# A two-model transformer block on one Trainium2 core: vector-engine order in the third and last mixers

## The reference

```python
# third mixer, per head (4 heads of 512 channels), written by chunks of 64 tokens in the reference
num = einsum(q k^T * w_intra, v) + w_inter * (C q)
den = s.sum(-1) + w_inter * (n . q)
h = num / max(|den|, exp(-m_row))
hn = (h - mean(h)) * rsqrt(var(h) + eps)
y = (hn * ln_w + skip * x_conv) * silu(z)
x = x + y @ w_out

# last mixer, 16 heads of 64 channels
q, k_c, v_c, k_s, v_s, k_w, v_w, z, g_logit = split(h @ w_in)
o = gate0 * o_cmp + gate1 * o_sel + gate2 * o_win      # three softmax attentions
x = x + (o * silu(z)) @ w_out
```

## Time and profile before

| | |
|---|---|
| median of 3 runs | 944.97 us (944.79 to 946.65) |
| the profiled execution | 943.69 us, its span 942.0 us |
| PE busy | 929.2 us, 99% of the span |
| DVE, ACT, POOL busy | 661.7, 531.6, 79.0 us |
| granted TensorE clock | 0.998 |
| chain that ended last | PE 85%, DVE 9%, ACT 3% |

### The profile page before, as it was taken

How to read it: one execution, slowest core, us unless ns; L and a number is a source line. 1 busy time by engine, 2 the same in 40 slices (tenths; PEclk the granted TensorE clock), 3 DMA queues, 4 the chain that set the end, 5 groups by cost and what they waited for, 6 DMA issues and landing times.

```text
span 942.0 us, 16082 instructions
## 1 busy us (share of the span) xinstructions
PE 929.2 (99%) x5908; PEld 813.3 (86%) x5908; DVE 661.7 (70%) x1107; ACT 531.6 (56%) x946; POOL 79.0 (8%) x104
## 2 busy tenths in 40 slices
PE   9999999999999999999999999999999999999997
PEld 9999888888888987888888888999888789999885
DVE  4978667555464897665545466997778876689985
ACT  6654465444444677654445446666545754377783
POOL 0000011111110000100000000000010006522200
PEclk9999999999999999999999999999999999999999
DMA  8655557656555323766555543533222575322312
GB/s 319 219 189 180 201 185 234 213 178 228 200 197 194 115 88 112 258 214 208 213 180 190 193 166 122 179 136 134 69 90 90 198 271 185 128 80 100 111 46 90
DMA packets 43692, 157.78 MB, mean 168 GB/s; under 512 B 5468, under 2 KB 6252, under 8 KB 42864
## 3 DMA queue, kind: packets, MB, share of 16 engines
q1 hardware_dynamic: 41664, 147.99, 45.3%
q0 software_dynamic: 1824, 8.45, 2.6%
q10 hardware_dynamic: 144, 0.52, 0.2%
HBM read 155.50 MB, written 1.05 MB: 166 GB/s over the span
## 4 chain that ended last, share of the span: by engine, by line
PE 85%; DVE 9%; ACT 3%; issue 1%; DMA 0%; POOL 0%; ACTq 0%; SPq 0%; DVEq 0%
PE ps L758 9%; PE ps L762 9%; PE ps L760 8%; PE ps L537 8%; PE ps L590 7%; PE ps L538 7%; PE ps L539 7%; PE ps L594 7%; PE ps L592 7%; DVE wl L1741 2%; PE ps L575 1%; PE ps L773 1%; PE ps L577 1%; PE ps L579 1%; PE ps L1124 1%
## 5 line engine op out<-in xcount | busy, mean ns | idle before, releaser
L1741 DVE TENSOR_TENSOR wl<-raw,wh 128x1024 fp32r<-128x1024 f32 x270 | 330.5, 1241 | 108.1 <-ACT wh L1210 59.9
L1210 ACT ACTIVATE wh<-raw 128x1024 fp32r<-128x1024 f32 x174 | 181.9, 1057 | 105.5 <-DMA raw<-stream_dram 90.6
L537 PE MATMUL ps<-hxa,wh 128*128 128x256 f32 x672 | 196.5, 292 | 1.1 <-DVE nq L1791 0.8
L538 PE MATMUL ps<-hxa,wh 128*128 128x256 f32 x672 | 189.9, 283 | 0.0
L539 PE MATMUL ps<-hxa,wl 128*128 128x256 f32 x672 | 189.8, 282 | 0.0
L758 PE MATMUL ps<-wh,hxa 128*128 128x512 f32 x352 | 139.1, 395 | 0.0
L762 PE MATMUL ps<-wl,hxa 128*128 128x512 f32 x352 | 137.3, 390 | 0.0
L537 PEld LDWEIGHTS ps<-hxa,wh 128*128 128x128 f32 x672 | 128.4, 191 | 10.1 <-issue 5.4
L760 PE MATMUL ps<-wh,hxa 128*128 128x512 f32 x352 | 137.0, 389 | 0.0
L1378 ACT ACTIVATE wh<-raw 128x1024 fp32r<-128x1024 f32 x96 | 100.0, 1058 | 50.9 <-DMA raw<-stream_dram 33.3
L538 PEld LDWEIGHTS ps<-hxa,wh 128*128 128x128 f32 x672 | 128.6, 191 | 0.1
(11 more groups left out here) (364 smaller groups left out, 1288.5 us busy)
## 6 DMA issues: line engine op xcount, KB each, us to landing
raw<-stream_dram SPq DMA_DIRECT2D x271, 512.0 KB, 4.0
biasm<-bias_dram POOLq DMA_DIRECT2D x12, 192.0 KB, 3.7
w<-w_dram POOLq DMA_DIRECT2D x1, 2048.0 KB, 10.6
mlw<-mlw_dram POOLq DMA_DIRECT2D x1, 1056.0 KB, 6.5
x<-x_dram SPq DMA_DIRECT2D x1, 1024.0 KB, 7.0
mem<-memT_dram SPq DMA_DIRECT2D x1, 1024.0 KB, 8.2
memx<-mem_dram SPq DMA_DIRECT2D x1, 1024.0 KB, 6.0
grow<-rows_dram POOLq DMA_DIRECT2D x2, 512.0 KB, 3.8
```

The costliest lines, as they stand in the source:

```text
L537: pe.matmul(o, wh[:, w_s, w_cols], act[hi], start=start, stop=False, skip_group_check=True)
L538: pe.matmul(o, wh[:, w_s, w_cols], act[lo], start=False, stop=False, skip_group_check=True)
L1210: act.activation(wh[:, v % RING, :], raw[:, v % RAW, :], ACT.Copy).then_inc(wh_ready, 1)
L1741: dve.tensor_tensor(wl[:, s % RING, :], raw[:, s % RAW, :], wh[:, s % RING, :].bitcast(F32), ALU.subtract).then_inc(wl_ready, 1)
```

## The change

It moves instructions on DVE and ACT and adds none; PE's and SP's programs are the same.

- Third mixer, DVE: for h = 2 the two operations of the denominator stand directly behind the decays of head 3, ahead of `low` and `take` of chunk z 9, the low parts of y and `weigh(3)`. In the last head `gated(4, 7)` and `gated(7, 9)` become `gated(4, 8)` and `gated(8, 9)`: the step c = 7 stands ahead of the reciprocal of line 2280.
- Last mixer, DVE: what stood at the end of pair p (an `ahead`, and the low part of y(p-2) for p of 2 and more) becomes `n_behind(p)`, called for p = 1 to 4 in the pair behind, between its two `n_maxima`. For p = 5 it stays at the end.
- Last mixer, ACT: in pair 0 `n_window(0)` and `n_window(1)` stand ahead of the `split` of line 1210.

```diff
@@ ACT
+                if p == 0:
+                    n_window(0)
+                    n_window(1)
                 for e in N_FILL[p][1:2]:
                     ahead_of(PN[e], e)
-                if p < N_PAIRS - 1:
+                if 0 < p < N_PAIRS - 1:
                     n_window(2 * p)
-                n_window(2 * p + 1)
+                if p:
+                    n_window(2 * p + 1)
@@ DVE, third mixer (denominator(h) is the block removed below)
                 if h + 1 < ML_HEADS:
                     decays(h + 1)
+                if h == 2:
+                    denominator(h)
                 if 1 <= h < ML_HEADS - 1:
                     gate_chunks(*Z_BEFORE[h])
@@
                 if h + 1 < ML_HEADS:
                     weigh(h + 1)
 
-                dve.wait_ge(ml_rows_copied, h + 1)
-                dve.wait_ge(ml_summed, h + 1)
-                link(dve.tensor_tensor(h_a[:], ps[:, 4, 0:T], h_em[:, h % 2, :], ALU.max))
-                e = dve.scalar_tensor_tensor(out=h_a[:], in0=ps[:, 4, 0:T], scalar=-1.0, in1=h_a[:],
-                                             op0=ALU.mult, op1=ALU.max)
-                e.then_inc(ml_den_ready, 1)
+                if h != 2:
+                    denominator(h)
                 dve.wait_ge(ml_den_ready, h + 1)
                 link(dve.reciprocal(h_r[:], h_a[:]))
@@
                 if h == ML_HEADS - 1:
-                    gated(4, 7)
+                    gated(4, 8)
                 dve.wait_ge(ml_std_ready, h + 1)
                 link(dve.reciprocal(h_a[:], h_t[:]))
                 if h == ML_HEADS - 1:
-                    gated(7, 9)
+                    gated(8, 9)
@@ DVE, last mixer
+            def n_behind(p):
+
+                ahead(PN["q", p + 2].u if p < 3 else PN["z", p].u)
+                if p >= 2:
+                    low_part(n_y[:], p - 2, Y_N + p - 2)
+
@@
                 n_maxima(2 * p)
+                if 2 <= p <= 5:
+                    n_behind(p - 1)
                 n_maxima(2 * p + 1)
@@
                     n_probs(2 * p + 1)
-                    ahead(PN["q", p + 2].u)
                 else:
@@
                     n_probs(2 * p + 1)
-                    ahead(PN["z", p].u)
-                if p >= 2:
-                    low_part(n_y[:], p - 2, Y_N + p - 2)
+                if p == 5:
+                    n_behind(p)
```

More of the change, by code:

```diff
@@ L2233, in add_skip, with denominator @@
                 dve.tensor_tensor(xc, xc, h_sq[:], ALU.add).then_inc(ml_done, 1)
+            def denominator(h):
+                dve.wait_ge(ml_rows_copied, h + 1)
+                dve.wait_ge(ml_summed, h + 1)
+                link(dve.tensor_tensor(h_a[:], ps[:, 4, 0:T], h_em[:, h % 2, :], ALU.max))
+                e = dve.scalar_tensor_tensor(out=h_a[:], in0=ps[:, 4, 0:T], scalar=-1.0, in1=h_a[:],
+                                             op0=ALU.mult, op1=ALU.max)
+                e.then_inc(ml_den_ready, 1)
             take(PM["z", 2], z_of(2), Rm)
```

## The result

| | before | changed |
|---|---|---|
| median | 944.82 us (8 runs) | 947.47 us (8 runs, 947.28 to 948.13) |
| ratio to before | | 1.0026, 95% interval 1.0017 to 1.0034 |
| the profiled execution | 943.69 us, span 942.0 | 947.45 us, span 945.7 |

The change makes the kernel slower by 0.26%, 2.65 us. The forecast was 948.7 in a range of 945.7 to 950.6, with 0.75 for slower.

The account below looks back on a forecast made before the run. PE, busy 99% of the span, bounds the kernel, so only its stalls can change. Gains 0.43, 0.50 and 0 against loss 4.63 add 3.70 to 944.97: 948.7 us, 8-in-10 range 945.7 to 950.6.

Parts of the forecast that it names:

- Part 4: Last mixer, `n_behind` between the two maxima: lengthens the stretch from scores to take of q in four pairs, loss 4.63 us.
- The lower bound for the split: Last mixer: four splits at 1.13 us each, less 0.91 given back, 3.6 us; the long row of 1.75 gave the upper.
- Part 3: Last mixer, first pair's windows scaled earlier: the 0.57 us wait returns at z(1), gain 0, bounds 0 and 0.57.
- Part 1: Third mixer, denominator of head 2 first: `ml_part(2)` stops waiting, DVE then binds `ml_part(3)`, gain 0.43 us, bounds 0 and 1.62.
- Part 2: Third mixer, step c = 7 ahead of the reciprocal: output unit 6's stall goes, gain 0.50 us, bounds 0.1 and 0.7.
- The sum: Whole kernel: gains 0.43, 0.50 and 0 against loss 4.63, +3.70 us on the median of 944.97, forecast 948.7.
- The range by the bounds: Whole kernel: from 944.97 + 3.6 - 2.3 = 946.3 to 944.97 + 5.7 - 0.1 = 950.6 us.
- (a): Rival, last mixer: DVE's lateness was the true bound, so waits for q vanish, 942.3 us; chance 0.08.
- (b): Rival, last mixer: half the block is hidden, the take not always being z(p)'s last need, 945.9 us; chance 0.12.
- (c): Rival, both mixers: gains come in full, 2.69 us against the loss of 4.63, 946.9 us; chance 0.06.
- (d): Rival, last mixer: later loads delay ACT's copies and exponentials, 1 us in each of two pairs, 950.7 us; chance 0.08.
- (e): Rival, third mixer: no gain, another wait replaces each, 949.6 us; within the forecast's range and its shared chance 0.66.

Follow-up runs that it names:

- the double block: Changed kernel with the blocks of pairs 2 and 3 behind the next pair's take of q, pair 4's back at pair 4's end: 945.38 us, 1.0010 of before.
- the low parts: Parts 1 to 3 of the change, with only the low parts of y(0) to y(2) moved behind the take of q in the next pair: 943.77 us, 0.9990.
- part 1 alone: Kernel before with only the third mixer's denominator of head 2 moved ahead, directly behind the decays of head 3: 943.28 us, 0.9984.
- the second profile of the kernel: Kernel before, unchanged, profiled once more: 945.36 us, 1.67 more than its first profile.
- the run with one block: Changed kernel with `n_behind` between the maxima in pair 2 only, in pairs 3 to 5 where it was before: 944.72 us, 0.9995 of before.
- the block behind the take: Changed kernel with `n_behind` in the same pairs, but behind the take of q(p+2) instead of between the two maxima: 946.98 us, 1.0018 of before.
- the run of parts 1 to 3: Changed kernel with `n_behind` put back at the end of its own pair, all other moves kept: 942.90 us, 0.9978 of before.
- the run of part 4 alone: Kernel before with only `n_behind` moved between the two maxima of the pair behind: 949.58 us, 1.0045.
- part 2 alone: Kernel before with only step c = 7 of `gated` moved ahead of the reciprocal: 944.75 us, 0.9999.

## Why the prediction was right, and where its terms were off

**Part 4, loss 4.63, measured 4.57.** From z(1) to z(5) it is 46.03 us before and 50.65 after, 4.62. The step was: the period is the stretch scores, maxima, take, z, scores; the block is put into it four times, and what DVE was late before is given back. Both terms show. The distance of two scores was 11.27 wherever the first maxima came 1.97 behind the scores, and longer by their lateness elsewhere: 0.82 late (2.79 behind) in pair 4, 11.27 + 0.82 = 12.09 (12.08 measured); 0.14 late in pair 3, 11.41 (11.40). After, the maxima come 1.96 or 1.97 behind in pairs 2 to 5, and the distances are 11.27 + 1.13 = 12.40 (12.41) and 11.27 + 1.47 = 12.74 (12.74 to 12.75). The same rule gives every distance of pairs 2 to 6 in the experiments that left the take where it was: the double block's 3.74 - 1.97 = 1.77 late is 13.04 (13.04), the low parts' 1.43 late is 12.70 (12.70). With the take 0.38 earlier, ahead of the shift, it holds less these 0.38: 3.80 - 1.97 = 1.83 late in pair 4 is 11.27 + 1.83 - 0.38 = 12.72 (12.72). The lower bound for the split, 1.13 and not 1.7, was the right one: at 849.76 it meets no POOL work.

**Part 3, gain 0, measured 0.04.** As told: z(1) waits for the take of q(3) instead, 0.43 on PE and 0.67 on its weight load, where I had 0.6.

**Part 1, gain 0.43, measured 1.29.** The mechanism at `ml_part(3)` was right, its size nearly; what came behind it was missed. At `ml_part(3)` it gained 0.54 in the changed kernel (606.94 behind line 606's first group, 607.48 before). I took DVE's idle time ahead of the take of z from the bracket, 0.60. The row ahead of that take, in the kernel before, is

```profile
722.01 1.22 DVE L2233 TENSOR_TENSOR skipx<-skipx,h_sq 128x1024 f32<-128x1024 f32 x1
```

and from start to start the idle time is 723.83 - 722.01 - 1.13 = 0.69, the way it counts for the operations behind it. In the changed kernel this row starts 0.16 later (601.14 behind line 606's first group, 600.98 before; I had 0.17): 0.53. The larger miss is behind that. Unit 6's stall, which I gave to part 2, goes with part 1 alone: ACT in head 3 follows PE's values and not DVE, so its first copy comes 1.50 and its square root 1.32 us earlier, DVE no longer idles 0.78 us for that copy, the reciprocal is 1.31 earlier, and that is more than the 1.18 by which y(6) had to come earlier.

**Part 2, gain 0.50, measured 0 on top of part 1 and 0.08 alone.** This step failed, and its result lies outside the bounds that I gave it (0.1 and 0.7). I took the stall of unit 6 as part 2's to remove and had shown only that units 7 and 8 stay within 0.1 us of late. With part 1 the stall is not there any more; without it, it moves to units 7 and 8. The stall was also larger than 0.50, for the quarter behind it took 0.80 us (745.23 to this row of the kernel before) instead of 0.68:

```profile
746.03 0.39 PE L590 MATMUL ps<-wh,y 128*128 128x512 f32 x1
```

So the third mixer gained 1.29 where the two terms had 0.93. That is right in sum to 0.36 and wrong in whose gain it was; that a term too small by 0.86 and one too large by 0.50 partly cancel is luck.

**The sum.** -1.29 - 0.04 + 4.62 = +3.3 against +3.70. From line 606's first group to the end of the span the changed kernel takes 824.28 us and the one before 820.94, 3.34 more. The medians are only 2.65 apart. The changed kernel's profile, whose time is that of its median, started 0.42 us later than the profile of the kernel before; if the median run of the kernel before (944.82, its profile 943.69) differs from its profile in the start alone, it started 1.13 later than 121.03. No trace shows that run, so this is inferred; the second profile of the kernel, 1.78 later at its start and 1.67 longer, shows that such starts occur. I had added the difference to the median of before, 944.97, as if the start were late by the same 1.28 in both. Of the error of 1.2 us, 0.36 is the third mixer's, and the rest, by this inference, is mostly the start. The range by the bounds has a slip that nothing hung on: its lower end takes off 2.3 us of gains (1.62 + 0.7) and leaves out the 0.57 that part 3 was allowed, and with it would be 945.7.

**The rivals.** (a), DVE's lateness as the true bound: it would have begun at a lateness of 1.13 us, and the largest was 0.82. (b), half of the block hidden: the run with one block excludes it, 1.13 for 1.13. (c), gains in full: 1.33 of its 2.69 came. (d), later loads: no distance holds any of it. (e), third mixer without a gain: excluded.

## What to carry to other kernels

Where two engines hand work to each other in a ring, price a move by asking on which arc of the ring the operation lands: between the producer's event and the hand-over it costs its whole length in every turn, and off that arc nothing (11.27 us in pair 2 with the block behind the take), until the engine's own sum per turn comes late to the next event; count the pairs into which a shifted block falls twice. Of two edits that both could remove a stall, run each alone, for the stall belongs to the earlier one if that makes everything behind it earlier. The best version here is the changed kernel without part 4: 942.90 us, 0.9978 of before. The runs do not tell it from part 1 alone (0.9984, and 194.35 and 75.34 us in the two mixers against 194.33 and 75.30).

## What the runs showed of the hardware that I had not expected

- A small DVE operation with two inputs in SBUF that starts under a product of POOL ends only behind it, whatever its own length: 0.22 became 0.80 us (line 2394, where POOL's took 0.73), 0.42 became 0.96 and 0.98 (low part, gate). Line 2442, with one of its inputs in PSUM, keeps its 0.42 under POOL's product (at 863.83 in the run of parts 1 to 3, POOL's from 863.60 to 864.40). Moving an operation by one place can push the next one into such a meeting, which cost more here than the move gained.
- Behind a standstill of 3.06 us PE was granted 0.50 of its clock from 902 to 904 us and 0.68 in the mean of the next 2 us, and lost 1.35 us more. It is one trace. From 20 us to PE's last instruction no other wait in any profile lowered the clock, up to 1.71 us ahead of z(5) in the run with pair 4's block back and 2.10 us at 23.78 in the run of part 4 alone.
- PE's start behind a late operand was slow by itself: the first quarter behind the stall of unit 6 took 0.80 us instead of 0.68, and so did those of units 7 and 8 with part 2 alone. What makes it so stays open.
